# The two halves of U 96 bytes, the parameters 128 bytes further into each partition

## The reference, cut to what matters

```python
for layer in range(DEPTH):                       # 2
    shift, scale, gate = ada_mod(c, ada_w[layer, 0], ada_b[layer, 0])
    u = x * (1.0 + scale) + shift
    y = even_mixer(u, ...) if layer % 2 == 0 else fox_attention(u, ...)
    x = layer_norm(ALPHA * x + gate * y, ln_g[layer, 0], ln_b[layer, 0])
    shift, scale, gate = ada_mod(c, ada_w[layer, 1], ada_b[layer, 1])
    u = x * (1.0 + scale) + shift
    y = jnp.square(jax.nn.relu(u @ mlp_w1[layer] + mlp_b1[layer])) @ mlp_w2[layer] + mlp_b2[layer]
    x = layer_norm(ALPHA * x + gate * y, ln_g[layer, 1], ln_b[layer, 1])
...
mix = _token_mixing(x, w_in, b_in, ...)
x = _layernorm(DEEPNORM_ALPHA * x + mix, ln1_g, ln1_b)
ffn = _conv_ffn(x, w_up, conv_f_w, conv_f_b, w_down)
x = _layernorm(DEEPNORM_ALPHA * x + ffn, ln2_g, ln2_b)
```

## Time and profile before

| | before |
|---|---|
| median of 3 executions | 4192.61 us |
| lowest and highest | 4184.55 and 4200.64 us |
| profiled execution, its own time | 4186.48 us |
| its span in the profile | 4184.7 us |
| mean granted TensorE clock | 0.968 |

### The profile page before, as it was taken

One profiled execution on the slowest core, in us unless ns is written; L12 is line 12 of the kernel. 1 busy time (PEld: TensorE's weight loads), 2 busy tenths in 40 slices (PEclk: granted clock), 3 DMA queues, 4 the chain that ended last, 5 costly groups with the idle time before them and its releaser, 6 DMA issues.

```text
span 4184.7 us, 50589 instructions
## 1 busy us (share of the span) xinstructions
PE 3908.5 (93%) x18934; PEld 3168.1 (76%) x18934; DVE 2069.1 (49%) x3073; ACT 1175.8 (28%) x1891; POOL 1918.4 (46%) x748
## 2 busy tenths in 40 slices
PE   6899899999999999999997999999999889999997
PEld 5677777888877777777775777777877667888886
DVE  6864564344354645545546422111479675444445
ACT  5322231111114444444432211111223242222222
POOL 2543286665554322222212774455464475445352
PEclk9999999999999999999988999999999999999999
DMA  6311013223211111011101111111111111111111
GB/s 217 117 56 33 19 51 96 89 88 102 81 46 31 36 36 35 27 31 36 36 21 31 41 56 45 40 45 55 41 35 52 41 51 51 44 46 50 40 60 40
DMA packets 246709, 224.65 MB, mean 54 GB/s; under 512 B 12916, under 2 KB 194834, under 8 KB 246563
## 3 DMA queue, kind: packets, MB, share of 16 engines
q1 hardware_dynamic: 222496, 171.09, 13.5%
q10 hardware_dynamic: 24067, 51.53, 3.8%
HBM read 218.33 MB, written 4.26 MB: 53 GB/s over the span
## 4 chain that ended last, share of the span: by engine, by line
PE 80%; DVE 13%; ACT 3%; issue 2%; DMA 1%; ACTq 0%; SPq 0%; DVEq 0%
PE PS L658 11%; PE PS L660 10%; PE PS L659 10%; PE PS L788 6%; PE PS L790 5%; PE PS L789 5%; PE PS L685 3%; PE PS L687 3%; PE PS L686 3%; PE PS L1143 3%; DVE ADMS L2130 2%; PE PS L1128 1%; PE PS L1113 1%; PE PS L1055 1%; PE PS L1075 1%
## 5 line engine op out<-in xcount | busy, mean ns | idle before, releaser
L3063 POOL TENSOR_SCALAR WH<-RAW 128x1024 fp32r<-128x1024 f32 x255 | 731.9, 2870 | 1293.6 <-PE PS L687 512.0
L658 PE MATMUL PS<-UH,WH 128*128 128x512 f32 (+1 forms) x2192 | 877.8, 400 | 13.4 <-DVE UL L2184 3.5
L659 PE MATMUL PS<-UL,WH 128*128 128x512 f32 (+1 forms) x2192 | 871.0, 397 | 0.0
L660 PE MATMUL PS<-UH,WL 128*128 128x512 f32 (+1 forms) x2192 | 871.0, 397 | 0.0
L3065 POOL TENSOR_TENSOR WL<-RAW,WH 128x1024 fp32r<-128x1024 f32 x255 | 622.7, 2442 | 21.3
L2141 DVE TENSOR_TENSOR X<-PS,X 128x512 f32<-128x512 f32 x432 | 292.7, 687 | 432.5 <-PE PS L790 421.4
L658 PEld LDWEIGHTS PS<-UH,WH 128*128 128x128 f32 (+1 forms) x2192 | 413.5, 189 | 120.0 <-issue 5.9
L660 PEld LDWEIGHTS PS<-UH,WL 128*128 128x128 f32 (+1 forms) x2192 | 412.6, 188 | 103.4
L659 PEld LDWEIGHTS PS<-UL,WH 128*128 128x128 f32 (+1 forms) x2192 | 413.2, 189 | 100.1 <-issue 0.2
L788 PE MATMUL PS<-WH,HH 128*128 128x512 f32 x1024 | 405.6, 396 | 26.2 <-DVE X L2141 13.4
L790 PE MATMUL PS<-WL,HH 128*128 128x512 f32 x1024 | 400.6, 391 | 0.0
(11 more groups left out here) (364 smaller groups left out, 7167.5 us busy)
## 6 DMA issues: line engine op xcount, KB each, us to landing
RAW<-in_mlp_w_dram SPq DMA_DIRECT2D x128, 512.0 KB, 3.9
ADM<-in_ada_w_dram ACTq DMA_DIRECT2D x96, 256.0 KB, 3.2
RAW<-in_w_up_dram SPq DMA_DIRECT2D x44, 512.0 KB, 3.8
ADR<-in_ada_w_dram ACTq DMA_DIRECT2D x32, 512.0 KB, 4.0
RAW<-in_w_down_dram SPq DMA_DIRECT2D x22, 512.0 KB, 3.5
RAW<-in_ev_w_in_dram SPq DMA_DIRECT2D x20, 512.0 KB, 3.9
RAW<-in_w_in_dram SPq DMA_DIRECT2D x20, 512.0 KB, 4.0
ADS<-in_ada_w_dram SPq DMA_DIRECT2D x16, 512.0 KB, 8.9
```

Source lines behind the costliest of these rows:

```text
L658: pe.matmul(bank(b)[0:width], wh, xh, start=(k == 0), stop=False)
L659: pe.matmul(bank(b)[0:width], wh, xl, start=False, stop=False)
L660: mm = pe.matmul(bank(b)[0:width], wl, xh, start=False, stop=(k == NK - 1))
L3063: pool.tensor_scalar(WH[slot][:, 0:n], r[:, 0:n], 1.0, None, ALU.mult).then_inc(S("w_hi"), 1)
```

## The change

UH and UL, and with them the ADS tiles that share their room, move 96 bytes up. The parameters, the weight slots and all that lies behind them move 128 bytes up, which makes room for that. Afterwards UH and UL are at 96, and the parameters, the weights and all other tiles are where they were within 128 bytes. X stays. The distance from UH to the first weight slot was 73440 bytes and is 73472, which is 224 and 256 modulo 512. Every engine's list of instructions is the same as before, row for row; only addresses differ.

```diff
         X = at("X", [P, NT, D], base)
-        UH = at("UH", [P, NK, SEQ], base + 32 * KB, F32R)
-        UL = at("UL", [P, NK, SEQ], base + 64 * KB, F32R)
-        o = base + 96 * KB
+        u0 = base + 32 * KB + 96
+        UH = at("UH", [P, NK, SEQ], u0, F32R)
+        UL = at("UL", [P, NK, SEQ], u0 + 32 * KB, F32R)
+        small0 = base + 96 * KB + 128
+        o = small0
...
-        BST8 = at("BST8", [P, NT, 12], base + 96 * KB + 4 * 656)
-        MV8 = at("MV8", [P, NT, 2], base + 96 * KB + 4 * 752)
+        BST8 = at("BST8", [P, NT, 12], small0 + 4 * 656)
+        MV8 = at("MV8", [P, NT, 2], small0 + 4 * 752)
...
-        ADS = [[at(f"ADS{g}{i}", [P, 4, D], base + (32 * (i + 1) + 16 * g) * KB) for i in range(2)] for g in range(2)]
+        ADS = [[at(f"ADS{g}{i}", [P, 4, D], u0 + (32 * i + 16 * g) * KB) for i in range(2)] for g in range(2)]
```

## The result

| | before | after |
|---|---|---|
| median of 12 executions | 4191.47 us | 4157.66 us |
| lowest and highest | 4182.58 and 4201.95 us | 4148.89 and 4181.68 us |
| ratio, 95% interval | | 0.992, 0.9901 to 0.9939 |
| profiled execution, its span | 4186.48, 4184.7 us | 4158.31, 4156.6 us |
| mean granted TensorE clock | 0.968 | 0.965 |

The medians lie 33.8 us apart, faster by 0.8%. The forecast was 42 us, with 4145 in a range of 4118 to 4175.

The account below looks back on a forecast made before the run. TensorE, busy 93% of the span, was taken to bound it through matmul start-to-start distances. Terms 18.0 + 14.0 + 2.7 + 3.2 + 3.0 + 0 + 1.5 = 42.4 us off 4186.5 gave 4144.1, stated as 4145, range 4118 to 4175.

Parts of the forecast that it names:

- The pace: Back-to-back 512-column matmuls reading U: step falls from 233.4 ns to the down-projection's pace, counted as 6.7 ns each.
- slower rival: U's matmuls: a distance of 256 modulo 512 costs another step, 234 to 240 ns, adding 52 us, 4238; chance 0.07.
- nothing happens: U's matmuls: offset not the cause, perhaps partition halves or a longer period; 4187; chance 0.14 together with pace-without-time case.
- rival 1: All U matmuls: separate read ports give one pace, so moving U gains nothing; 4187; 0.14 including the pace-without-time case.
- The switches: Up- to down-projection: 7 steps no longer settle, 4 ns each, at 16 + 16 + 22 switches; 1.5 us saved.
- The MLPs: Up-projections of both MLPs: 3072 matmuls at 6.7 ns, 20.6 us, less 2.6 for HL waits; 18.0 us saved.
- I give back half over 8 groups: First MLP's waits for HL: half of each group's 0.64 us gain is lost, 2.6 us.
- The FFN: Up-projections of the last FFN: 2112 matmuls at 6.7 ns, 14.1 us, counted as 14.0 us saved.
- The first mixer: Recurrent/GLA mixer: 816 matmuls at 6.7 ns, 5.5 us, halved for waits on gates; 2.7 us saved.
- the spatial mixer: Spatial mixer: 960 matmuls at 6.7 ns, 6.4 us, halved for busy VectorE and lower clock; 3.2 us saved.
- 256 columns: 256-column products with U stationary, attention and line 673 with followers: between 0 and 7 us gain, taken as 0.
- The attention: Attention's q/k: 768 matmuls, 5.1 us at most, in pieces of 12 behind other work; 3.0 us saved.

Follow-up runs that it names:

- e1: Changed kernel with UH and UL back at 0, so only parameters and weights move 128 bytes, weights at 96; 4194.11 us, ratio to before 1.0008.
- e2: Changed kernel with UH and UL back at 0 and parameters and weights moved 32 bytes, so U and all weights lie at 0; 4154.2 us, ratio 0.9919.
- e3: Changed kernel with U at 32 and weights at 96, 64 bytes apart within 128; 4183.41 us, ratio to before 0.9991.
- e5: Changed kernel with U at 64 and weights at 96, 32 bytes apart within 128; 4188.04 us, ratio to before 0.9989.
- e6: Changed kernel with UH back at 0, UL alone at 96 and weights at 96; 4194.21 us, ratio to before 1.0007.
- e4: Changed kernel, with ScalarE in the first MLP making each hidden tile before issuing its modulation-sum loads; 4138.28 us, ratio to before 0.9863.
- e7: Kernel before, addresses unchanged, with only ScalarE's reordering in the first MLP: hidden tile first, then modulation-sum loads; 4172.14 us, ratio to before 0.9943.

## Why the prediction was right, and where it was too large

**The pace (right).** 233.4 to the down-projection's pace was forecast, 226.6 measured, with U moving and with U stationary. e1, e2, e3, e5 and the two rooms in e6 leave the shared offset as the cause: the same room of U at 0 gives 234 ns or 226.7 with the weights at 96 or at 0, and 32, 64 and 96 bytes of difference all give the long step. Both ways out that I had given a place fell: the distance of 256 modulo 512, which no row of before showed, costs nothing (no slower rival), and lower against upper half of the partition does not matter (no "nothing happens"). One point is not settled. In every pair with the short step the distance is a multiple of 256 bytes, and no kernel put two operands at an odd multiple of 128. The period can be 128 or 256 bytes. How the engine comes to it stays open too. The rule of read ports of their own in the Trainium skill ("TensorE: Matmul & The Clock Gate", Part 2) says nothing of addresses. As I read it in rival 1, it gave all these matmuls one pace, and here the pace depends on an address: 226.6 against 233.4 ns.

**The switches (right).** 1.5 us forecast. The 7 steps behind a switch now take 1.59 in place of 1.62 us, 0.03 us at 54 switches, 1.6.

**The MLPs.** The second: 10.3 forecast, 10.1 measured. In the first I had seen the wait for HL and gave back half of a half group's gain, 2.6 us. This is the term that failed: "I give back half over 8 groups". Measured, 4.3 us went into the seven waits, and two stretches at the 1.2 GHz level behind them cost some 1.6 us each. 10.3 less 4.3 less 3.2 is the 2.8 us that were left. I could have decided the first part beforehand, since the order of ScalarE's work was in the code and HL's spacing in the trace. VectorE *was* late, because of the round of loads, sums and ScalarE. e4 and e7 show it: with the round cut open, the addresses bring their 10.1 us. The sum had no term for the clock.

**The FFN.** 14.0 forecast, 12.9 measured. I had counted no wait there. TensorE's three long waits of this stage grew from 8.1, 5.5 and 2.9 us to 8.4, 6.0 and 3.1, 1.0 us together, which is about what is missing. The first mixer came out 1.5 us below the forecast, the spatial mixer 0.5 above.

**256 columns (wrong sign).** I took 0 between 0 and a gain. It was a loss. The products of one token item after another, first and last of 192, before and after:

```profile
410.88 0.28 PE L673 MATMUL PS<-WH,UL 128*128 128x256 f32 x1
...
433.48 0.28 PE L675 MATMUL PS<-WL,UH 128*128 128x256 f32 x1
```

```profile
410.18 0.28 PE L675 MATMUL PS<-WH,UL 128*128 128x256 f32 x1
...
433.09 0.28 PE L677 MATMUL PS<-WL,UH 128*128 128x256 f32 x1
```

191 steps in 22.60 and in 22.91 us, 118.3 and 119.9 ns. For 2304 of them that is 3.7 us lost, most of it in the attention. I had bounded this term from below at nothing, though no row excluded a loss. The nearest row (K and Q) did not carry over. The shared offset is not what costs here: e1, with 96 bytes of difference, has 120.0 ns as well. By W minus U modulo 512 the same 191 steps take 118.3 ns at 224, 119.9 at 256 (after and e2), 116.8 at 288 (e5), 117.8 at 320 (e3) and 120.0 at 352 (e1). What orders them stays open.

**The attention.** Forecast -3.0, in the two profiles +2.6. The loss above explains some 2.5 us of the 5.6 between them. The rest is within what the stage does on its own. Its length depends on how long TensorE's clock stays low, and that differs between kernels with the same instructions. From its first to its last matmul, before, after and e5:

```profile
1293.60:2252.50 958.90, 892.07 (x5320) 730.35 (x5320) 494.83 (x953) 408.63 (x702) 233.65 (x88) 0.96 0.10 30
```

```profile
1289.60:2251.10 961.50, 893.79 (x5319) 733.58 (x5320) 494.75 (x953) 408.54 (x702) 230.51 (x88) 0.96 0.10 30
```

```profile
1291.90:2279.10 987.20, 919.65 (x5320) 752.20 (x5320) 492.79 (x953) 408.92 (x702) 235.18 (x88) 0.93 0.10 30
```

e5's profiled execution is 28 us longer here than before's, with a clock of 0.93 against 0.96, while its median is like before's. In the traces the clock is at 1.2 GHz for 71.7 us of this stretch before, 75.1 after and 143.4 in e5. So a single profile says little on this stage. The scatter of whole executions goes with the clock: of the 27 executions of the kernel before that were timed beside e5, the shortest (4179.78 us) has a mean clock of 0.968 and the longest (4222.77 us) 0.958. That most of this arises in the attention was not tested.

**The sum.** 42.4 us forecast, 33.8 measured between the medians, and 28.1 between the two profiles. What the stages miss in the profiles: 4.9 us in the first MLP (1.7 more given back to HL, 3.2 to the low clock behind it), 5.6 in the attention, 1.5 in the first mixer and 1.1 in the FFN, with the loss at 256 columns, 3.7 us, spread over the attention and the mixers. The forecast of 4145 has a slip of its own. I took the 42.4 us off the profiled execution, 6 us below the median. Taken off the median of 4192.61 they give 4150, nearer to the measured 4157.66. That the time lay within the range is owed to the pace and to the width of the range; the sizes of two stages were off.

## What to carry to other kernels

Compare the distance between starts of matmuls of one shape across the kernel: where two groups differ by a few ns at the full clock, look at the offsets of the two operands. Here stationary and moving tiles in float32 words at one offset within 128 bytes saved 3% of each 512-column step, for 32 bytes of padding. The 256-column steps moved between 116.8 and 120.0 ns in another order, so each width has to be measured by itself. Before counting such a gain as time, follow the round that feeds the next wait: if that round does not contain the matmuls, the gain is waited away, and the longer wait may cost clock as well.

## What the runs showed of the hardware that I had not expected

- The pace of back-to-back 512-column matmuls with U moving takes only few values: 226.7 ns with one shared offset (96 or 0), 233.3 with 32 or 64 bytes of difference, 233.4 and 234.3 with 96 bytes at distances of 224 and 352 modulo 512. At the 1.2 GHz level there is no surplus over the columns.
- Which operand plays which role matters at 64 bytes: 233.3 ns with U moving, 229.0 with U stationary.
- At 256 columns the address of U against W counts too, from 116.8 to 120.0 ns, but not by the shared offset: 119.9 ns with it (after and e2), 120.0 without (e1), 116.8 to 118.3 in e5, e3 and the kernel before.
- An idle stretch of 1.82 us in an otherwise busy TensorE was followed by 3.4 us at the 1.2 GHz level, where 1.34 us at the same place was not. Of six such stretches of 1.8 us in the changed kernel's first MLP, two were followed by the lower level.
